# Experts' down product as three one-pass products of split halves, norm weights multiplied into the stored rows, and a pair's products in another order

## The reference

```python
def hierarchical_moe(h, r_grp, r_exp, w_gate, w_up, w_down):
    t = h.reshape(B * S, D)                      # 512 x 1024
    ... # gates: each token takes 2 of 16 experts
    a = jnp.einsum("td,edf->tef", t, w_gate)     # 1024 -> 512
    u = jnp.einsum("td,edf->tef", t, w_up)
    hid = jax.nn.silu(a) * u * gates[:, :, None]
    y = jnp.einsum("tef,efd->td", hid, w_down)   # 512 -> 1024

h = rms_norm(x, ffn_norm[l])     # x / rms(x) * ffn_norm[l]
x = x + hierarchical_moe(h, router_group[l], router_expert[l], w_gate[l], w_up[l], w_down[l])
```

## Time and profile before

| what | value |
|---|---|
| runs | 1744.4, 1737.7 and 1742.4 us, median 1742.4 |
| profiled execution, span from first to last instruction | 1741.3 us (the page gives no other time of it) |
| busy: PE, DVE, ACT, POOL | 1524.0, 1106.7, 664.3, 389.1 us |
| mixture of layer 0 | about 250 to 663 us |
| mixture of layer 1 | about 1334 to 1739 us |

### The profile page before, as it was taken

The page is one execution under the profiler, slowest core; times in us unless marked ns, Lnnn a source line. Parts: engine busy times, 40 slices in busy tenths (PEclk is TensorE's granted clock), DMA queues, the critical chain, the costliest instruction groups (busy, mean ns, idle before and its releaser), DMA issues. The chain is left out here.

```text
span 1741.3 us, 19609 instructions
## 1 busy us (share of the span) xinstructions
PE 1524.0 (88%) x7176; PEld 1191.2 (68%) x7176; DVE 1106.7 (64%) x1372; ACT 664.3 (38%) x686; POOL 389.1 (22%) x340
## 2 busy tenths in 40 slices
PE   6889584899999973999999999999988399999991
PEld 5778374667676742788888888888876376767660
DVE  6886625665566637777757677586743665666653
ACT  4110712455555524323243232423332245554531
POOL 4100001132222213413314133140400222222220
PEclk9989895899999995999999999999999599999996
DMA  4214422388888826212112121121213658888854
GB/s 175 83 65 152 159 85 112 128 352 350 362 350 371 356 98 237 85 49 72 60 60 84 36 84 60 60 75 46 73 64 134 263 215 361 346 366 347 341 203 169
DMA packets 52050, 308.72 MB, mean 177 GB/s; under 512 B 10288, under 2 KB 16048, under 8 KB 38192
## 3 DMA queue, kind: packets, MB, share of 16 engines
q1 hardware_dynamic: 34304, 284.98, 41.4%
q0 software_dynamic: 9648, 16.80, 2.7%
q10 hardware_dynamic: 8064, 6.50, 1.2%
HBM read 298.28 MB, written 28.31 MB: 188 GB/s over the span
## 5 line engine op out<-in xcount | busy, mean ns | idle before, releaser
L632 POOL TENSOR_TENSOR KQ<-rope_ab 64x512 f32<-64x512 f32 x96 | 173.3, 1805 | 390.7 <-DVE rope_ab L1332 387.1
L1241 DVE TENSOR_TENSOR wgl<-WR,wgh 128x2048 fp32r<-128x2048 f32 x66 | 148.2, 2287 | 173.2 <-ACT wgh L786 170.3
L1567 PE MATMUL PS<-WR,SC 128*128 128x512 f32 x528 | 233.2, 594 | 3.4 <-ACT SC L820 1.6
L852 ACT ACTIVATE wh<-wraw 128x1024 fp32r<-128x1024 f32 x80 | 84.4, 1058 | 274.8 <-PE PS L1627 252.1
L1567 PEld LDWEIGHTS PS<-WR,SC 128*128 128x128 f32 x528 | 98.8, 190 | 117.3 <-issue 115.3
L1241 DVE TENSOR_TENSOR wul<-WR,wuh 128x2048 fp32r<-128x2048 f32 x66 | 148.0, 2283 | 0.5 <-ACT wuh L786 0.4
L786 ACT ACTIVATE wgh<-WR 128x2048 fp32r<-128x2048 f32 x66 | 122.4, 1904 | 61.0 <-DMA WR<-w_gate 61.0
L786 ACT ACTIVATE wuh<-WR 128x2048 fp32r<-128x2048 f32 x66 | 122.7, 1906 | 31.1 <-PE PS L1541 17.0
L1332 DVE TENSOR_TENSOR rope_ab<-PS,rope_sb 32x512 f32<-32x512 f32 x192 | 131.9, 687 | 2.6
L1313 DVE TENSOR_TENSOR wl<-wraw,wh 128x1024 fp32r<-128x1024 f32 x80 | 97.8, 1225 | 49.8 <-ACT wh L852 48.0
L1539 PE MATMUL PS<-wgh,xgh 128*128 128x512 f32 x264 | 111.6, 423 | 5.2 <-DVE xgl L1259 5.2
(11 more groups left out here) (260 smaller groups left out, 3334.0 us busy)
## 6 DMA issues: line engine op xcount, KB each, us to landing
WR<-w_gate SPq DMA_DIRECT2D x33, 2048.0 KB, 12.4
WR<-w_up SPq DMA_DIRECT2D x33, 2048.0 KB, 16.7
WR<-w_down SPq DMA_DIRECT2D x33, 2048.0 KB, 12.6
wraw<-w_qkv SPq DMA_DIRECT2D x72, 512.0 KB, 3.3
WR<-w_in SPq DMA_DIRECT2D x8, 1024.0 KB, 4.9
WO<-w_out SPq DMA_DIRECT2D x1, 4096.0 KB, 15.8
xn_dram<-HTQ SPq DMA_DIRECT2D x8, 512.0 KB, 2.7
HT<-y_dram SPq DMA_DIRECT2D x8, 512.0 KB, 6.6
```

The costliest lines, as they stand in the source:

```text
L632: nc.gpsimd.tensor_tensor(to, cos, sin, ALU.add).then_inc(rope_done, 1)
L852: nc.scalar.activation(wh[:, s, :], wraw[:, s, :], ACT.Copy).then_inc(wh_done, 1)
L1241: V.tensor_tensor(lo[:, kts, :], raw[:, kts, :], hi[:, kts, :].bitcast(F32), ALU.subtract).then_inc(done, 1)
L1567: ins = M.matmul(PS[3 + h][:, :], hidT[:, ft, :], wd[b][:, ft, h * 512:(h + 1) * 512], start=ft == 0, stop=ft == FT - 1)
```

## The change

- **Down product.** ACT splits w_down as well (`down_lead`, two instructions of 128x2048, into one buffer `wdh`), DVE subtracts (`down_trail`, two), and the transposed hidden rows are split too (`hidden_lead` on ACT and `hidden_trail` on DVE, in place of `copy_hidT`). `down` becomes 24 one-pass products; its first half waits for the first half of the split weights, its second half for the second.
- **Norm weights.** DVE multiplies them into the normalised rows before these are stored (one instruction with two factors in place of L934, with `gain_row`, one row broadcast to all partitions by a DMA). `copy_xgT` goes; `rows_lead` and `rows_trail` read PSUM, in two halves each, and slot 1 gets banks of its own (7 and 1). Because bank 1 is that of up, up(0) waits for `rows_trail(1)`.
- **Order.** PE: gate(0), up(0), first half of gate(1), transpose hidden(0), second half of gate(1), down(0), up(1), transposes of rows(0), hidden(1), rows(1), down(1). ACT and DVE: as in the diff.
- Small tables that routing leaves for the loop move out of the place where `wdh` lies.

```diff
+ROW_BANKS = ((5, 6), (7, 1))
...
+        wdh = at("wdh", 32, [P, FT, D], F32R)
+        wdl = [at(f"wdl{b}", 112 + 16 * b, [P, FT, D], F32R) for b in range(2)]
+        hTh, hTl = at("hTh", 188, [P, FT, P], F32R), at("hTl", 190, [P, FT, P], F32R)
...
+            sp.dma_start(gain_row, a["ffn_norm"][0].to_broadcast([P, D])).then_inc(row_in.sem, 16)
             expert_load(0, 1, 1, wu, "w_up", wu_in)
...
+                def down_lead(b, n):
+                    act.wait_ge(wd_in[l][b], n * 16)
+                    for q in range(2):
+                        fts = slice(q * FT // 2, (q + 1) * FT // 2)
+                        nc.scalar.activation(wdh[:, fts, :], wd[b][:, fts, :], ACT.Copy).then_inc(dh_done[l], 1)
                 def rows_lead(b, n):
-                    act.wait_ge(xgT_done[l][b], n)
-                    nc.scalar.activation(xgh[b][:, :, :], xgT[b], ACT.Copy).then_inc(xh_done[l], 1)
+                    act.wait_ge(xgT_mm[l][b], n)
+                    for q in range(2):
+                        nc.scalar.activation(xgh[b][:, 4 * q:4 * q + 4, :], PS[ROW_BANKS[b][q]][:, :].rearrange("p (a b) -> p a b", a=4),
+                                             ACT.Copy).then_inc(xh_done[l], 1)
                 gate_lead(0, 1, None)
                 up_lead(0, 1, None)
                 for b in range(2):
                     rows_lead(b, 1)
+                act.wait_ge(gl_done[l], 2)
+                down_lead(0, 1)
...
+                    def hidden_lead(b):
+                        act.wait_ge(hT_mm[l], 2 * i + (b + 1))
+                        nc.scalar.activation(hTh[:, :, :], PS[2][:, :].rearrange("p (a b) -> p a b", a=FT), ACT.Copy).then_inc(hTh_done[l], 1)
                     silu_gate(0)
                     if more:
                         gate_lead(1, i + 1, 2 * i + 1)
                         up_lead(1, i + 1, 2 * i + 1)
+                        hidden_lead(0)
                         silu_gate(1)
                         gate_lead(0, i + 2, 2 * i + 2)
+                        store_y(0)
+                        down_lead(1, i + 1)
                         rows_lead(0, i + 2)
+                        hidden_lead(1)
                         up_lead(0, i + 2, 2 * i + 2)
-                        store_y(0)
                         rows_lead(1, i + 2)
                         store_y(1)
+                        down_lead(0, i + 2)
                     else:
                         with act.If(two > 0):
                             gate_lead(1, i + 1, 2 * i + 1)
                             up_lead(1, i + 1, 2 * i + 1)
+                        hidden_lead(0)
+                        with act.If(two > 0):
                             silu_gate(1)
                         store_y(0)
                         with act.If(two > 0):
+                            down_lead(1, i + 1)
+                            hidden_lead(1)
                             store_y(1)
...
+                        V.scalar_tensor_tensor(XN[k][:, n, :], X[:, n, :], rstd[:, one], gain_row, ALU.mult, ALU.mult).then_inc(xn_ready.sem, 1)
...
-                def copy_xgT(b, n):
-
-                    dve.wait_ge(xgT_mm[l][b], n)
+                def down_trail(b, m):
                     for q in range(2):
-                        ins = V.tensor_tensor(xgT[b][:, 4 * q:4 * q + 4, :], PS[5 + q][:, :].rearrange("p (a b) -> p a b", a=4),
-                                              gain[:, 4 * q:4 * q + 4].rearrange("p (a o) -> p a o", o=1).to_broadcast([P, 4, P]), ALU.mult)
-                    ins.then_inc(xgT_done[l][b], 1)
+                        fts = slice(q * FT // 2, (q + 1) * FT // 2)
+                        dve.wait_ge(dh_done[l], 2 * m + (q + 1))
+                        V.tensor_tensor(wdl[b][:, fts, :], wd[b][:, fts, :], wdh[:, fts, :].bitcast(F32), ALU.subtract).then_inc(dl_done[l], 1)
                 def rows_trail(b, m):
-                    dve.wait_ge(xh_done[l], m + 1)
-                    V.tensor_tensor(xgl[b][:, :, :], xgT[b], xgh[b][:, :, :].bitcast(F32), ALU.subtract).then_inc(xl_done[l], 1)
+                    for q in range(2):
+                        dve.wait_ge(xh_done[l], 2 * m + (q + 1))
+                        ins = V.tensor_tensor(xgl[b][:, 4 * q:4 * q + 4, :], PS[ROW_BANKS[b][q]][:, :].rearrange("p (a b) -> p a b", a=4),
+                                              xgh[b][:, 4 * q:4 * q + 4, :].bitcast(F32), ALU.subtract)
+                    ins.then_inc(xl_done[l], 1)
                 gate_trail(0, 0)
-                for b in range(2):
-                    copy_xgT(b, 1)
                 for b in range(2):
                     rows_trail(b, b)
                 up_trail(0, 0)
+                down_trail(0, 0)
...
-                    def copy_hidT(b):
-                        dve.wait_ge(hT_mm[l], 2 * i + (b + 1))
-                        if b == 1:
-                            dve.wait_ge(down_mm[l], 2 * i + 1)
-                        V.tensor_copy(hidT.rearrange("p a b -> p (a b)"), PS[2][:, :]).then_inc(hidT_done[l], 1)
+                    def hidden_trail(b):
+                        dve.wait_ge(hTh_done[l], 2 * i + (b + 1))
+                        V.tensor_tensor(hTl[:, :, :], PS[2][:, :].rearrange("p (a b) -> p a b", a=FT), hTh[:, :, :].bitcast(F32),
+                                        ALU.subtract).then_inc(hTl_done[l], 1)
                     if more:
                         gate_trail(1, 2 * i + 1)
                         hidden(0)
                         up_trail(1, 2 * i + 1)
-                        copy_hidT(0)
-                        copy_xgT(0, i + 2)
+                        hidden_trail(0)
                         gate_trail(0, 2 * i + 2)
+                        down_trail(1, 2 * i + 1)
+                        hidden(1)
+                        hidden_trail(1)
                         rows_trail(0, 2 * i + 2)
-                        hidden(1)
-                        copy_hidT(1)
                         up_trail(0, 2 * i + 2)
-                        copy_xgT(1, i + 2)
                         rows_trail(1, 2 * i + 3)
-                        dve.wait_ge(down_mm[l], 2 * i + 2)
+                        down_trail(0, 2 * i + 2)
                     else:
                         with dve.If(two > 0):
                             gate_trail(1, 2 * i + 1)
                         hidden(0)
                         with dve.If(two > 0):
                             up_trail(1, 2 * i + 1)
-                        copy_hidT(0)
+                        hidden_trail(0)
                         with dve.If(two > 0):
+                            down_trail(1, 2 * i + 1)
                             hidden(1)
-                            copy_hidT(1)
+                            hidden_trail(1)
...
-                    if b == 1 or not isinstance(n, int):
-                        pe.wait_ge(xgT_done[l][1 - b], n - 1 if b == 0 else n)
                     for kt in range(KT):
-                        ins = M.transpose(PS[5 + kt // 4][:, (kt % 4) * P:(kt % 4 + 1) * P], xg[b][:, kt::KT], ident[:, :])
+                        ins = M.transpose(PS[ROW_BANKS[b][kt // 4]][:, (kt % 4) * P:(kt % 4 + 1) * P], xg[b][:, kt::KT], ident[:, :])
                     ins.then_inc(xgT_mm[l][b], 1)
...
                         if b == 1:
                             pe.wait_ge(sil_done[l], 2 * i + 1)
-                        project(PS[0][:, :], b, 2 * i + b, wgh, wgl[b], gl_done[l]).then_inc(gate_mm[l], 1)
+                        pe.wait_ge(xl_done[l], 2 * i + (b + 1))
+                        project(PS[0][:, :], b, 2 * i + b, wgh, wgl[b], gl_done[l], range(KT // 2))
+                        if b == 1 and more:
+                            transpose_hidden(0)
+                        project(PS[0][:, :], b, 2 * i + b, wgh, wgl[b], gl_done[l], range(KT // 2, KT)).then_inc(gate_mm[l], 1)
                     def up(b):
+                        if b == 0:
+                            pe.wait_ge(xl_done[l], 2 * i + 2)
                         project(PS[1][:, :], b, 2 * i + b, wuh, wul[b], ul_done[l]).then_inc(up_mm[l], 1)
...
-                        pe.wait_ge(wd_in[l][b], (i + 1) * 16)
-                        pe.wait_ge(hidT_done[l], 2 * i + (b + 1))
+                        pe.wait_ge(hTl_done[l], 2 * i + (b + 1))
                         pe.wait_ge(y_done[l], 2 * i + (b + 1))
-                        for h in range(2):
-                            for ft in range(FT):
-                                ins = M.matmul(PS[3 + h][:, :], hidT[:, ft, :], wd[b][:, ft, h * 512:(h + 1) * 512],
-                                               start=ft == 0, stop=ft == FT - 1)
+                        for ft in range(FT):
+                            if ft % (FT // 2) == 0:
+                                pe.wait_ge(dl_done[l], 2 * (2 * i + b) + (ft // (FT // 2) + 1))
+                            for h in range(2):
+                                cols, dst = slice(h * 512, (h + 1) * 512), PS[3 + h][:, :]
```

(49 more changed lines are left out.)

20 lines of the change are left out of this document (12 added, 8 removed).

## The result

The changed kernel takes **1780.5 us** (median of four runs, 1778.5 to 1781.2) where the kernel before takes 1742.9 beside it (1737.7 to 1744.4): a ratio of 1.0219, 95% interval 1.0204 to 1.0235, +37.6 us. The profiled span went from 1741.3 to 1779.3, +38.0. The forecast was 1773, with a range from 1753 to 1808: the direction and most of the amount came as predicted, and 7.5 us were not foreseen.

The account below looks back on a forecast made before the run. PE alone was taken to bound the loop before, the chain between engines after. Terms 21.8 - 3.4 + 6.1 + 2.6 - 0.9 + 4.2 = +30.4 put the span at 1771.7; forecast 1773 us, range 1753 to 1808.

Parts of the forecast that it names:

- the loop: Slot loop: an iteration goes from 38.95 to 40.4 us, +1.45, in 15 iterations +21.8 us.
- The chain: One loop iteration, hand to hand between PE, ACT and DVE from the end of down(1): 40.4 us, PE standing twice.
- never stops: Loop of the kernel before: PE busy 39.10 of 39.10 us, so whatever ACT and DVE need is hidden.
- rival C: Clock falls in the loop's new gaps: +3.1 us in each iteration hit, 1819 us in all, 1788 in a third; chance 0.15.
- signs of being wrong: PE busy through an iteration, a granted clock under 1.00 in the loop, or store_y waiting for POOL.
- The last pair: End of layer 1: 15.3 us becomes 21.4, +6.1, plus 2.6 for 12 of down(1)'s products at half the clock.
- The start: Start of each layer: gate(0) no longer waits for slot 1's rows, -1.7 us a layer (bounds 0 and -2.6), -3.4 together.
- The norms: Norm in both layers: the two-factor DVE instruction costs 0.53 us more in each of four tiles a layer, +4.2 us.
- A: Loop: PE stays the bound, ACT's and DVE's part fitting into 36.0 us an iteration; 1706 us; chance 0.07.
- B: Loop: hand-offs of nothing and no late silu, an iteration of 39.3 us or less; 1756 us; chance 0.13.
- D: Loop: a scatter landing 3 us past 21 us after its issue delays store_y(0) and all behind; +45, 1818 us; chance 0.05.
- POOL pays, DVE never: When POOL's SBUF reads meet DVE's subtractions, only POOL waits; otherwise up to 1.7 us more where DVE waits.

Follow-up runs that it names:

- ht_first: Changed kernel with hidden_trail(0) moved ahead of up_trail(1) in DVE's list in the loop; 1755.5 us, ratio 1.0075.
- d_first: Changed kernel with down_lead(1) moved ahead of store_y(0) in ACT's list in the loop; 1760.0 us, ratio 1.0102.
- both_first: Changed kernel with hidden_trail(0) ahead of up_trail(1) on DVE and down_lead(1) ahead of store_y(0) on ACT, in the loop; 1732.1 us, ratio 0.9942.
- no_sub: Changed kernel without down_trail, PE multiplying the high half of w_down a second time instead; only its time is of use; 1742.5 us, ratio 1.0000.
- fill: Changed kernel with seven unneeded one-pass products before the transposes of hidden(1) in the loop; 1773.2 us, ratio 1.0171.
- last_pair: Changed kernel with the loop's order in the last pair too, and there down_lead(1) ahead of store_y(0) on ACT; 1773.5 us, ratio 1.0175.
- start_wait: Changed kernel with one more PE wait ahead of the loop, on the split of slot 1's rows; 1783.5 us, ratio 1.0239.
- norm_only: Kernel before with the norm part alone: weights multiplied into the stored rows, copies without a scale; 1747.5 us, ratio 1.0028.
- order_only: Kernel before, float32 down product kept, with only the changed kernel's order on PE, ACT and DVE; 1814.1 us, ratio 1.0423.
- old_order: Changed kernel with PE's order of before, rows' copies moved forward to match, splits and one-pass down products kept; 1834.0 us, ratio 1.0522.
- best: Changed kernel with hidden_trail(0) ahead of up_trail(1), down_lead(1) ahead of store_y(0), and down(0) ahead of up(1) in the last pair; 1729.4 us, ratio 0.9919.

## Why the prediction was right, and where it was short

| stage | forecast | measured (profiles) |
|---|---|---|
| norms and routing, both layers | +4.2 | +5.1 |
| first rows' transposes to first w_down issue, both layers | -3.4 + 2 x 1.45 = -0.5 | -1.8 - 1.2 = -3.0 |
| 12 iterations between | 12 x 1.45 = +17.4 | 12.2 + 11.4 = +23.6 |
| layer 0: last iteration and last slot | 1.45 - 0.9 = +0.6 | +1.05 |
| layer 1: last pair | +8.7 | +8.65 |
| everything else | 0 | +2.6 |
| sum | +30.4 | +38.0 |

The sum came nearer than its parts: the loop cost 6.2 more than forecast, and the start gave 2.5 more than forecast, which hid part of that. This was luck.

**The chain.** Its steps against the undisturbed iteration, from the end of down(1) (0.2 before 395.98): silu(0) 6.3 forecast, 6.2 measured; first down product 18.95, 18.8; end of down(0) 24.4, 24.4; `down_trail(1)` 27.5, 27.5; transposes of hidden(1) 32.7, 32.7; down(1) 34.9, 34.8; whole 40.4, 40.40. PE stands for 1.65 and 2.0 us where I had 2.1 and 2.0. The new forms cost what their nearest rows cost: `hidden_lead` 0.60, `hidden_trail` 0.69; the down product 5.6 for 5.44 (from 414.57 to the first of up(1) at 420.16). ht_first, d_first, both_first and no_sub moved it by the forecast amounts within 0.1. This part is shown. Two of its premises are less exact: PE "never stops" before, but every second iteration there has short gaps of 0.2 to 1.0 us; and the hand-offs agree as a sum, not each by a run of its own.

**The term that was mis-sized** is the loop: +1.45 an iteration against +1.97 (23.6 / 12). All that was missing is the clock's, which I had as rival C with 0.15; a granted clock under 1.00 in the loop was one of my own signs of being wrong, and it showed (0.96 in eight of twelve iterations). 40.4 less the 39.05 of before would be +1.35, and the falls add 0.9 to 1.1 in two of three. fill shows both. I took C's price too high and its chance too low. The price was 3.1 with twelve cold products and late transposes. Measured is about 0.95: the eight transposes of rows go from 1.06 to 1.71 but end inside the wait for the hidden rows, down(1) starts on time (471.00 is 40.40 after 430.60), and four or five products run cold before the clock is back. The chance was low because the earlier trace rows had 1.00 behind a gap of 1.81. But one such row says that it can stay up, not that it does: behind the same 1.79 it fell in 8 of 12 here and in 6 of 12 in each of ht_first, last_pair and start_wait. The row was not quite alike either. Behind its 1.81 PE ran a product, while here eight transposes stand ahead of the gap and four behind it. No run tells which of this matters, nor why one iteration is hit and the next is not.

The Trainium skill (TensorE: Matmul & The Clock Gate, "A second HAM failure mode: psum-queue depth-cycling") says that short idle times between groups of products can make the clock go back and forth, each time with a cost. By it, gaps of 2 us in every iteration should have been suspected; the traces agree, with half the clock behind gaps of 1.8 us, and show none behind those of 0.87.

**The last pair** came out at 8.65 for 8.7, but as a sum: the cold products are ten (from 1734.94 to 1739.37), about 2.1 us in place of 2.6, and the rest, 6.5 in place of 6.1, is the chain's.

**The start** gave more than -1.7 a layer: -3.0 for both, and this includes the first iteration's own loss of about 1.35 each, so nearly -2.9 a layer. The bound of -2.6 was too tight; gate(0) follows 1.6 us behind the start of slot 1's transposes where it took 4.6. start_wait shows 3 us of the 5.7 in both layers as the wait on slot 1's rows; the rest (no `copy_xgT` in the way) was not tried.

**The norms** stand by norm_only. That the profiles give 5.1 has another part: the router's 64 small products of layer 1 took 11.39 us before, 12.02 in norm_only and 13.29 after, at mean clocks of 0.61, 0.58 and 0.52. **Everything else** is +2.6, of which 1.9 lie ahead of the first changed instruction: the first norm of layer 0 begins at 251.4 before, and at 253.9 in order_only, which has the same instructions up to there. So the change does not make it, and I take it for scatter between executions. Where the other 0.7 lies I did not look into.

**Rivals.** A is refuted: PE has gaps in every version, also at 37.7 (36.3 busy). B: the undisturbed iteration is 40.40 and not 39.3. D: the wait for the scatter ended at 410.6 and store_y(0) began at 420.4; 8.6 us of room behind POOL's instruction of 1.1, where I had 3.5, because the scatter landed 12.8 after its issue and not 17.8.

**The port.** "POOL pays, DVE never" holds for the loop and not beyond it. In the changed kernel DVE's subtractions of 128x2048 in the loop stayed within 2277 and 2300 ns, and one took 2351 in old_order. POOL's read behind the scatter (L600) went from 253 ns on average to 1479, but another of its small reads (L570 before, L588 after) went from 1020 to 188, and its three small reads together took 47.7 us before and 49.6 after. In the first layer, in this kernel and in the one before, DVE does pay, beside a long POOL instruction:

```profile
25.67 23.49 POOL L555 TENSOR_TENSOR X<-X,WR 128x1024 f32<-128x1024 f32 x4 [24.50 <-DVE HTal L998]
```

```profile
38.30 3.53 DVE L1007 TENSOR_TENSOR wil<-WR,wih 128x2048 fp32r<-128x2048 f32 x1
```

The same subtraction took 2.28 to 2.29 in its seven other places. The Trainium skill (SBUF — State Buffer, "Who interferes with whom") has whoever comes second wait. The traces agree that either side can be the one that loses. That the loser waits for the whole of the other's instruction they don't show: DVE lost 1.2 us here beside POOL instructions of 5.9 us each (four in 23.49). The prediction read one side from rows in which POOL's reads were short.

## What to carry to other kernels

Before work is taken off the engine that bounds a loop, write down the chain through the others from the end of one product to the start of the next: here a handful of rows gave 40.4 us to the tenth, where PE's own list said 36. Then look at each list for the instruction that stands behind one nobody waits for yet: two such lines, moved, turned a ratio of 1.0219 into 0.9942, part of it through the clock. And price each new gap of PE twice, once as time and once as clock.

## What was not expected of the hardware

- A gap of 1.79 us, with transposes around it, brings the clock down in half to two thirds of otherwise equal iterations; 0.87 never did, in four kernels. In best's last pair, gaps of 1.76 and 1.41 with four transposes between kept it at 0.50 for 6.5 us; in last_pair, with the same gaps, it was there for 3.5.
- In the changed kernel's loop the clock was at 0.50 for about 3.4 us each time. What a fall cost depends on what stood in those 3.4 us: 0.9 to 1.1 here, where part of them is a wait for other engines, and 1.7 in order_only.
- Products that compute nothing are worth issuing: seven in each iteration gave 7 us back, twelve in the last pair about 3 (2.8 in that pair's profile).
- The kernel before, too, has iterations of two kinds (38.5 and 39.0 to 40.2, in turn) at a clock of 1.00 throughout. In the long ones PE waits 0.2 to 1.0 us for `hidden` ahead of hidden(1)'s transposes and in some up to 0.36 for y behind them. What starts it I did not look into.
